# Group norm behind the RWKV scan: two sets of banks, full-width gate products, sample columns apart, and an earlier receptance in each scan step

## The reference

```python
g = jax.nn.sigmoid(xg @ g1) @ g2                 # g1: 1024 x 128, g2: 128 x 1024
...
def step(S, inp):                                # one token, one 64 x 64 state per head
    r_t, w_t, k_t, v_t, kk_t, a_t = inp
    sa = jnp.einsum('bhvk,bhk->bhv', S, -kk_t)
    S = (S * w_t[:, :, None, :] + sa[..., None] * (kk_t * a_t)[:, :, None, :]
         + v_t[..., None] * k_t[:, :, None, :])
    return S, jnp.einsum('bhvk,bhk->bhv', S, r_t)
S, y = lax.scan(step, S0.astype(jnp.float32), (tm(rh), tm(decay), tm(kh), tm(vh), tm(kk), tm(ah)))
mean = jnp.mean(y, axis=-1, keepdims=True)       # group norm: over the 64 columns of a head
var = jnp.mean(jnp.square(y - mean), axis=-1, keepdims=True)
y = ((y - mean) * lax.rsqrt(var + RWKV_GN_EPS)).reshape(B, T, D)
y = y * lnx_w.astype(jnp.float32) + lnx_b.astype(jnp.float32)
bonus = jnp.sum(rh * kh * r_k.astype(jnp.float32), axis=-1, keepdims=True) * vh
y = y + bonus.reshape(B, T, D)
out = (y.astype(x.dtype) * g) @ w_o
```

## Time and profile before

| | |
|---|---|
| median of three runs | 3455.47 us |
| profiled execution, whole / its span | 3454.23 us / 3452.5 us |
| TensorE matmul, weight load, busy | 3105.7 us (90%), 2896.8 us (84%) |
| VectorE, ScalarE, GpSimd busy | 1585.1, 1075.7, 1314.6 us |
| scan's end to first output product | about 1315 to 1418.65 us of the span |
| key products L719 on GpSimd, from 1320 | 8 x 1.281 us |
| scalings L1199, squares L1204 on ScalarE | 8 x 0.715, 8 x 0.637 us |
| split L1210 on ScalarE, L725 on GpSimd | 8 x 0.637, 8 x 1.290 us |
| last `ct` of the scan on GpSimd ends | 1308.3 us |

### The profile page before, as it was taken

How to read it: one execution, slowest core, us unless ns; L and a number is a source line. 1 busy time by engine, 2 the same in 40 slices (tenths; PEclk the granted TensorE clock), 3 DMA queues, 4 the chain that set the end, 5 groups by cost and what they waited for, 6 DMA issues and landing times. The chain is left out here.

```text
span 3452.5 us, 76015 instructions
## 1 busy us (share of the span) xinstructions
PE 3105.7 (90%) x30651; PEld 2896.8 (84%) x30651; DVE 1585.1 (46%) x2423; ACT 1075.7 (31%) x2057; POOL 1314.6 (38%) x910
## 2 busy tenths in 40 slices
PE   6998999948979997889999896778999989999997
PEld 6997999838968885779999694667999979889997
DVE  3437662092047773276620203435664153476622
ACT  3224332243242222143322326024333232243321
POOL 3443444434313332334444231233444424434442
PEclk9998999969969997789999897688999989989998
DMA  7542334504500001123345352022333535323332
GB/s 249 161 125 61 92 92 142 161 10 130 158 31 3 3 3 47 49 62 92 92 142 159 104 162 82 0 80 62 92 92 119 172 117 170 110 63 92 92 90 75
DMA packets 462933, 331.56 MB, mean 96 GB/s; under 512 B 19786, under 2 KB 433432, under 8 KB 462434
## 3 DMA queue, kind: packets, MB, share of 16 engines
q1 hardware_dynamic: 453400, 317.63, 30.2%
q10 hardware_dynamic: 9322, 10.77, 1.0%
HBM read 318.57 MB, written 10.20 MB: 95 GB/s over the span
## 5 line engine op out<-in xcount | busy, mean ns | idle before, releaser
L609 POOL TENSOR_TENSOR w_lo<-w_raw,w_hi 128x1024 fp32r<-128x1024 f32 x406 | 1024.7, 2525 | 1147.9 <-ACT w_hi L775 1147.8
L1354 PE MATMUL bank<-u_hi,w_hi 128*128 128x260 f32 (+1 forms) x4240 | 872.2, 287 | 48.2 <-ACT w_hi L775 25.1
L1354 PE MATMUL bank<-u_lo,w_hi 128*128 128x260 f32 (+1 forms) x4240 | 862.1, 285 | 0.0
L1354 PEld LDWEIGHTS bank<-u_hi,w_hi 128*128 128x128 f32 (+1 forms) x4240 | 652.2, 189 | 71.0 <-issue 45.1
L1354 PEld LDWEIGHTS bank<-u_lo,w_hi 128*128 128x128 f32 (+1 forms) x4240 | 656.2, 189 | 1.9
L775 ACT ACTIVATE w_hi<-w_raw 128x1024 fp32r<-128x1024 f32 x406 | 428.6, 1056 | 487.5 <-PE bank L1360 194.2
L1360 PE MATMUL bank<-u_hi,w_lo 128*128 128x260 f32 (+1 forms) x4240 | 552.0, 283 | 0.0
L1360 PEld LDWEIGHTS bank<-u_hi,w_lo 128*128 128x128 f32 (+1 forms) x4240 | 525.1, 187 | 1.8
L1354 PE MATMUL bank<-hid_hi,w_hi 128*128 128x260 f32 x1664 | 338.4, 285 | 0.0
L1354 PE MATMUL bank<-hid_lo,w_hi 128*128 128x260 f32 x1664 | 334.8, 283 | 0.0
L1354 PEld LDWEIGHTS bank<-hid_hi,w_hi 128*128 128x128 f32 x1664 | 256.2, 188 | 13.7 <-issue 12.3
(11 more groups left out here) (382 smaller groups left out, 4119.7 us busy)
## 6 DMA issues: line engine op xcount, KB each, us to landing
w_raw<-in_ffn_w_up_dram SPq DMA_DIRECT2D x176, 512.0 KB, 3.7
ada_raw<-in_ada_w_dram SPq DMA_DIRECT2D x168, 512.0 KB, 4.5
w_raw<-in_ffn_w_down_dram SPq DMA_DIRECT2D x64, 448.0 KB, 5.2
w_raw<-in_sconv_w_in_dram SPq DMA_DIRECT2D x48, 512.0 KB, 5.7
w_raw<-in_ffn_w_down_dram SPq DMA_DIRECT2D x32, 512.0 KB, 4.6
ada_pro<-in_ada_w_dram SPq DMA_DIRECT2D x6, 2048.0 KB, 20.6
w_raw<-in_rwkv_w_rkv_dram SPq DMA_DIRECT2D x24, 512.0 KB, 5.7
w_raw<-in_gla_w_in_dram SPq DMA_DIRECT2D x24, 512.0 KB, 5.3
```

The lines of the kernel that those rows point to most:

```text
L609: pool.tensor_tensor(w_lo[:, s, :, :], w_raw[:, s, :, :], w_hi[:, s, :, :].bitcast(F32), ALU.subtract).then_inc(lo_done, 1)
L1354: pe.matmul(tile_ps[slot][half][0:width, 0:HALF], w_hi[:, s, k, 0:width], x[:, k0 + k, half * HALF:(half + 1) * HALF], start=start and k = ...
```

## The change

**Scan steps.** `receptances` comes before the wait for the state products and gives its signal itself; the copy of `end_decay` stays behind the state update as a step of its own. The sample-state instructions move: two behind the last level, and three (q=0) or two (q=1) at the very end of a step.

**Scan's end.** GpSimd's key products wait only for the last receptance. ScalarE makes `bonus_ones`, eight matrices `pair_ones` scaled by `r_k`, in the last step, and r itself is no longer scaled. The two first mean products stand ahead of the transposes.

**Group norm.** Prompt and samples part: the prompt's 512 columns are one product into one bank, with two banks for the means and two for the bonus, and the eight tiles' sample columns (64 in all) go together in bank 5 with a few small instructions of their own. In the second pass the spread rows use four banks and run two tiles ahead of the gate products, which contract 128 rows at once: `g2` and `t_g` lie on 128 partitions, for which the second half of g1 is multiplied in a block of 128 columns (`w_raw` columns 64 to 127).

**DMA.** The outputs of the states are issued by SP instead of ScalarE, ahead of the output weights.

```diff
-                    for k in range(KT):
-                        pool.wait_ge(r_scaled, k + 1)
+                    pool.wait_ge(bd_ready, 2 * NCH)
+                    for k in range(KT):
                         pool.tensor_tensor(rw_r[:, k, :], rw_r[:, k, :], rw_k[:, k, :], ALU.mult).then_inc(rk_ready, 1)
...
+                            if not one_more and lvl < 4:
+                                for k in range(2 * lvl, 2 * lvl + 2):
+                                    ins = act.activation(bonus_ones[:, k, :], pair_ones[:, :], ACT.Copy,
+                                                         scale=vec("rwkv_r_k", k))
+                                if lvl == 3:
+                                    ins.then_inc(bonus_ready, 1)
                         act.wait_ge(u_mm, w + 1)
...
-                    act.wait_ge(st_updated, 2 * NCH + 2)
...
+                    for k in range(KT):
+                        act.wait_ge(centred, max(k + 2, 3))
...
                     pe.wait_ge(tile_free[1], t0 // 2 + 2)
-                    gemm(n0 + 3, 1, 1, u_hi, u_lo, 0, KT, True, True, width=HD)
+                    gemm(n0 + 3, 1, 1, u_hi, u_lo, 0, KT, True, True)
...
+
+                    def mean_of(k):
+
+                        if k >= 2:
+                            pe.wait_ge(centred, k - 1 + (k >= 4))
+                        pe.matmul(bank[k % 2][:, :], pair_ones[:, :], rw_y[:, k, 0:TP], start=True, stop=True)\
+                          .then_inc(mean_mm, 1)
...
+                    def bonus_of(k):
+
+                        pe.wait_ge(rk_ready, k + 1)
+                        if k >= 2:
+                            pe.wait_ge(ynorm_done, k - 1)
+                        pe.matmul(bank[2 + k % 2][:, :], bonus_ones[:, k, :], rw_r[:, k, 0:TP], start=True, stop=True)\
+                          .then_inc(bonus_mm, 1)
...
+                    def squares_of(k):
+
+                        pe.wait_ge(csq_done, k + 1)
+                        head_sums(bank[4], k, gn_tmp[:, k % 2, :]).then_inc(var_mm, 1)
...
+                    mean_of(0)
+                    mean_of(1)
                     pe.wait_ge(s_y_done, 1)
...
+                    bonus_of(0)
+                    pe.wait_ge(srow_copied, 7)
+                    pe.matmul(bank[5][:, 0:KT * NS], pair_ones[:, :], sample(rw_y), start=True, stop=True).then_inc(mean_mm, 1)
+                    bonus_of(1)
+                    for k in range(2, KT + 2):
+                        if k < KT:
+                            mean_of(k)
+                        squares_of(k - 2)
+                        if k < KT:
+                            bonus_of(k)
+                    for k in range(KT):
+                        mm = pe.matmul(bank[5][:, (KT + k) * NS:(KT + k + 1) * NS], bonus_ones[:, k, :], rw_r[:, k, TP:T],
+                                       start=True, stop=True)
+                    mm.then_inc(bonus_mm, 1)
...
+                    def spread_tile(k):
...
+                        if k >= 2:
+                            pe.wait_ge(ynorm_done, max(KT, KT + k - 2))
+                        for g in range(NG):
+                            n = min(TG, TP - g * TG)
+                            for i in range(2):
+                                c = g * QUAD + 2 * k + i
+                                mm = pe.matmul(bank[k % 4][i * HD:(i + 1) * HD, g * TG:g * TG + n],
+                                               ident[:, c:c + 1].to_broadcast([P, HD]), rstd[:, 0:n],
+                                               start=True, stop=True)
+                        mm.then_inc(var_mm, 1)
...
+                    pe.wait_ge(centred, KT + 2)
+                    spread_tile(0)
+                    spread_tile(1)
+                    spread_sample()
+                    pe.wait_ge(g2_loaded, 16)
+                    pe.wait_ge(ynorm_done, KT + 1)
+                    for k in range(KT):
+                        c0 = (3 * KT + k) * NS
+                        pe.matmul(bank[5][:, c0:c0 + NS], g2[:, k * P:(k + 1) * P], t_g[:, TP:T], start=True, stop=True)
                     pe.wait_ge(wkv_copied, 1)
...
+                    for k in range(KT):
                         if k >= 2:
                             pe.wait_ge(gated, k - 1)
-                        for half in range(2):
-                            for i in range(2):
-                                mm = pe.matmul(bank[4 + 2 * (k % 2) + half][:, 0:HALF], g2[:, i, k * P:(k + 1) * P],
-                                               t_g[:, i, half * HALF:(half + 1) * HALF], start=(i == 0),
-                                               stop=(i == 1))
-                        mm.then_inc(g_mm, 1)
+                        pe.matmul(bank[6 + k % 2][:, :], g2[:, k * P:(k + 1) * P], t_g[:, 0:TP], start=True, stop=True)\
+                          .then_inc(g_mm, 1)
+                        if k + 2 < KT:
+                            spread_tile(k + 2)
...
                         b = bd[q]
                         dve.tensor_tensor(b["ZR"][:, :, HD:2 * HD], rw_r[:, 4 * q:4 * q + 4, ds(HD * c, HD)],
-                                          b["Ep"][:, :, 1:HD + 1], ALU.mult)
-                        dve.tensor_copy(end_decay[:, q, :], b["Ep"][:, :, HD:HD + 1].rearrange("p i a -> p (i a)"))\
-                           .then_inc(bd_ready, 1)
+                                          b["Ep"][:, :, 1:HD + 1], ALU.mult).then_inc(bd_ready, 1)
+
+                    def end_decays(q):
+
+                        return dve.tensor_copy(end_decay[:, q, :], bd[q]["Ep"][:, :, HD:HD + 1].rearrange("p i a -> p (i a)"))
...
                                 mask_scores(w + 1, 1 - q, lvl)
-                            if lvl in (0, 4):
-                                sample_state(c, 4 * q + q + (0, 0, 0, 0, 1)[lvl])
...
-                        sample_state(c, 5 * q + 2)
+                        for j in range(2):
+                            sample_state(c, 5 * q + j)
                         if one_more:
                             dve.wait_ge(u_mm, w + 1)
                             first_inverse(w + 1, 1 - q)
-                        sample_state(c, 5 * q + 3)
...
-                        if q == 0:
-                            sample_state(c, 4)
+                        if two_more:
+                            dve.wait_ge(y_mm, w + 1)
+                            receptances(c + 1, q)
                         dve.wait_ge(st_mm, w + 1)
...
                         ins.then_inc(st_updated, 1)
                         if two_more:
                             dve.wait_ge(st_updated, w + 3)
-                            receptances(c + 1, q)
+                            link(end_decays(q))
+                        for j in range(2, 4 + (q == 0)):
+                            sample_state(c, 5 * q + j)
...
-                    for k in range(KT + 1):
-                        if k < KT:
-                            dve.wait_ge(mean_mm, k + 1)
-                            for half in range(2):
...
+                    def centre(k):
...
+                        dve.wait_ge(mean_mm, k + 1 + (k >= 2))
+                        dve.scalar_tensor_tensor(rw_y[:, k, 0:TP], bank[k % 2][:, :], -1.0 / HD, rw_y[:, k, 0:TP],
+                                                 ALU.mult, ALU.add).then_inc(centred, 1)
...
+                    def value_bonus(k):
...
+                        dve.wait_ge(bonus_mm, k + 1)
+                        dve.tensor_tensor(rw_v[:, k, 0:TP], rw_v[:, k, 0:TP], bank[2 + k % 2][:, :],
+                                          ALU.mult).then_inc(ynorm_done, 1)
...
+                    centre(0)
+                    centre(1)
+                    dve.wait_ge(mean_mm, 3)
+                    dve.scalar_tensor_tensor(sample(rw_y), columns(5, 0), -1.0 / HD, sample(rw_y), ALU.mult, ALU.add)\
+                       .then_inc(centred, 1)
+                    value_bonus(0)
+                    for k in range(2, KT):
+                        centre(k)
+                        value_bonus(k - 1)
+                    value_bonus(KT - 1)
                     dve.wait_ge(gstd_done, 1)
                     dve.reciprocal(rstd[:, 0:TG], std[:, 0:TG]).then_inc(centred, 1)
...
+                    dve.tensor_tensor(sample(rw_v), sample(rw_v), columns(5, KT * NS), ALU.mult).then_inc(ynorm_done, 1)
+                    link(dve.tensor_tensor(sample(rw_y), sample(rw_y), per_tile("rwkv_lnx_w"), ALU.mult))
...
+                    def scaled(k):
...
+                        dve.wait_ge(var_mm, KT + k + 1 + (k >= 2))
+                        dve.scalar_tensor_tensor(rw_y[:, k, 0:TP], rw_y[:, k, 0:TP], vec("rwkv_lnx_w", k),
+                                                 bank[k % 4][:, :], ALU.mult, ALU.mult).then_inc(ynorm_done, 1)
...
+                    def gate_tile(k, behind):
...
+                        dve.wait_ge(dve_step, base[0] + step[0] - behind)
+                        dve.wait_ge(g_mm, k + 1)
                         if k >= 2:
```

(17 more changed lines are left out.)

155 lines of the change are left out of this document (59 added, 96 removed).

## The result

The changed kernel takes 3395.66 us, the median of four runs (3390.37 to 3399.73), against 3454.57 for the kernel before beside it: ratio 0.984, interval 0.9819 to 0.9862. The prediction was 3397. The runs of the kernel before lie apart too, in three groups (3443 to 3447, 3453 to 3456 and 3461 to 3462 us, with one at 3450); its profile is one of the middle group, and what sets the groups apart isn't known. The profiled execution has a span of 3398.0 us, 54.5 less than before.

What follows compares the result with a forecast made beforehand. Chains of waits in scan steps and both group norm passes, with TensorE often at 1.2 GHz, were taken as the bound; 5.9 + 55.9 + 1.0 - 4.5 - 0.5 = 57.8 us off 3455.5, said as 3397, range 3387 to 3415.

Steps and rivals of the forecast that it cites:

- likeliest case: Whole kernel: one fall of the clock in each pass, 3397 us, own range 3392 to 3403, chance 0.45.
- Scan steps: Scan: earlier receptance signal cuts TensorE's waits, seven pairs at 0.96 us, less 0.8 in the last step: 5.9 gained.
- The rival that the samples take the whole place: Scan: sample instructions hold up the first inverse addition as long as the old wait; scan gain 0, 3403 us, chance 0.12.
- First pass: Group norm's first pass: two bank sets break the ring, 2.40 us a tile against 4.16; second pass begins 20.0 us earlier.
- Ring kept: First pass: an overlooked wait keeps the ring, 13 of the 20 us stay away, 3410 us, chance 0.04.
- Second pass: Group norm's second pass: VectorE is the period, 2.25 us a tile; both passes gain 55.9 us at full clock.
- Contention: Scan's end: some six VectorE instructions slowed beside GpSimd's key products, up to 1.2 us, half on the chain: 0.5 charged.
- Clock in the passes: Both group norm passes: one fall of TensorE's clock in each, 4.5 us charged for both.
- the open point: Second pass: what brings TensorE's clock back; 64-row gate products may be what held it down. No size given.
- The rival of the second pass at 1.2 GHz: Second pass stays at 1.2 GHz: gain 44.5 us, 3411; with the first pass slow too, 3423; chance 0.22.
- Output start: Output product starts at the full clock: 1.0 us credited of a possible 2.9.
- no fall: Rival: the clock does not fall at all, 4.5 and 1.9 us more gained, 3391 us, chance 0.15.

Runs made afterwards that it cites:

- e0: The changed kernel run again unchanged on another chip, five executions: 3390.91 us against 3453.46 for the kernel before, ratio 0.982.
- e1: The changed kernel with VectorE's order in a scan step as before (receptances behind the state update, samples at old places): 3393.67 us, ratio 0.984.
- e3: The changed kernel with one bank for means and one for bonus in the first pass, instead of two each: 3404.74 us.
- e4: The changed kernel with GpSimd's eight key products started only behind the last state update: 3391.34 us.
- e7: The changed kernel with GpSimd writing zeros as the low part of the gated result and reading nothing: 3387.54 us.
- e2: The changed kernel with each gate product as two products of 64 rows (rows 0 to 63 twice): 3416.12 us.
- e5: The changed kernel with VectorE's second-pass order turned: gate product of tile k, shift of k+1, scaling of k+2: 3385.27 us, ratio 0.982.
- e6: The changed kernel with unread 128x512 products on TensorE, four before the scan's first scores, three behind the last gate product: 3389.01 us.

## Why the prediction was right

The likeliest case was 3397 with a gain of 57.8; the profiled execution gained 54.5 and e0's 63.3. The mechanisms of the gain are those of the prediction. Contention and the clock were sized wrong in opposite directions, and a late rise of the clock that it did not foresee stands in half of the first four runs.

- *Scan steps.* 0.96 a pair was worked out, 1.07 measured, and the new wait of 1.04 behind the samples stands where the step said. Behind steps with q=1, where the sum let the whole wait go, one of about 0.3 stays. The rival that the samples take the whole place falls. From the first to the last state update it is 4.6 (e0: 4.5) where 5.9 less the 0.5 for contention was worked out; in the first step the new order gives 1.0 more (29.4 us from the first scores to the first update in e1, 28.4 in e0), a place without a term. The last two steps lost 1.6 (31.1 to 32.7) where 0.8 and part of the contention were charged.
- *First pass.* 2.40 a tile was said, 2.28 measured, no fall of the clock. The second pass began at 1338.26, in the prediction 1337.7, although the last state update came 1.4 late: 22.2 us between the two, where 23.0 was worked out. "Ring kept" falls, and e3 shows what it would have cost.
- *Second pass.* Period 2.25 said, 2.04 where nothing disturbs. The first gating ended 8.7 behind the start of the first spread where 9.2 was worked out, the first output product 1.66 behind the last gating as said. End at 1363.97 instead of 1361.1.
- *Contention*, the term that was mis-sized: 0.5 was charged for six instructions at the scan's end. It cost 1.0 there (e4), and in the second pass three shifts at 1.1 more each, 3.4 (in e0's profile two), that had no term at all: the centring and the gates were looked at, which read PSUM, and the shift between them, which reads two SBUF tiles, was not. The rows agree with the rule of the Trainium skill that the prediction cites (SBUF — State Buffer, "Who interferes with whom"): the shift was long beside the low part, 1.86, and not beside the writes of e7, 0.75. The slip was to apply it to two of three instructions. The 0.88 of the earlier trace rows also was a poor bound: beside whole 520-column products the same form took 1.63.
- *Clock in the passes*, mis-sized the other way: 4.5 for two falls. One came, at 1342.8 for 3.7 us, behind the samples' 8-column products as was feared (in e0's profile none), and made the way from reciprocal to first gating 9.38 us against 8.43 in e0: 0.95. That 64-row gate products hold the clock down was the open point, and e2 bears it out for this place. The rival of the second pass at 1.2 GHz falls for the full products.
- *Output start.* 1.0 credited; in the changed kernel's profile it ran at 0.50 until 1370.2, and in e0's until 1361.3, while e5, e6 and e7 began at the full clock. The rest behind it is 1.5 and 0.5.
- *Not foreseen*: 9.0 us in some executions for a late rise of the clock in the scan's first step, a place which the prediction took as unchanged. Since before's runs lie apart too and only one of them has a profile, how often it had such executions isn't known. The late rise is why the median of the first four runs, two of each kind, fits 3397, and why e0's five fit the rival "no fall" (3391) better. The agreement to 1.3 us is in part luck.

## What to carry over

Where a stage is a ring over one buffer, price it by the ring and then by each engine's own work: both passes came out within 0.3 us a tile where no contention fell in. When an engine gets a new neighbour, go through every instruction that runs beside it for two SBUF inputs, not only the long ones, and try to turn the order so that the reading pairs miss each other; here that took a stretch of 23.6 us (e0, without a fall of the clock) to 20.3 (e5). A total that carries a clock's chance of 9 us doesn't judge an edit of 5: read the distance of two like rows.

## What the runs showed of the hardware

- VectorE's two-input SBUF instruction and GpSimd's ran almost one after the other: 0.75 and 1.27 became 1.86 and 1.27, VectorE's ending 0.55 behind GpSimd's, or 0.75 and 1.84, GpSimd's ending 1.14 behind VectorE's. The starts in the profile don't tell which will wait: VectorE's was first by 0.04 or 0.05 us in both cases (1349.71/1349.75, 1359.23/1359.28), and e0 has both outcomes at 0.05 (1341.04/1341.09, where GpSimd took 1.84, and 1343.08/1343.13, where VectorE took 1.86).
- A GpSimd instruction of 0.52 us that only wrote to SBUF cost VectorE's shift beside it nothing: 0.75 (e7).
- At 100% busy with gate products of 64 rows and the spread products between them, TensorE stayed at 1.2 GHz for 35 us (e2). It also stayed there for 10.5 us, 100% busy, with products of 128 rows and 64 columns (the changed kernel's first profile), where the same 48 records ran at 2.4 GHz in e0 (5.57 us).
